# A float32 decoder trunk on one Trainium2 core: the MLP's up-projection by pairs of tiles, in seven block products in place of eight

## What is computed

```python
h = rmsnorm(x, mlp_norm[l])
u = jnp.square(jax.nn.relu(jnp.einsum('bsd,df->bsf', h, w_up[l])))    # 1024 -> 4096
x = x + jnp.einsum('bsf,fd->bsd', u, w_down[l]).astype(x.dtype)       # 4096 -> 1024
```

## Time and profile before

| | before |
|---|---|
| median of 3 runs (lowest, highest) | 1188.17 us (1187.81, 1190.7) |
| span of the profiled execution | 1186.0 us |
| busy PE / DVE / ACT / POOL | 1154.9 / 538.6 / 590.7 / 574.1 us |
| MLP of layer 0, of layer 1 (about) | 243 to 592 us, 824 to 1177 us |

### The profile page before, as it was taken

The page is one execution under the profiler, slowest core; times in us unless marked ns, Lnnn a source line. Parts: engine busy times, 40 slices in busy tenths (PEclk is TensorE's granted clock), DMA queues, the critical chain, the costliest instruction groups (busy, mean ns, idle before and its releaser), DMA issues.

```text
span 1186.0 us, 15497 instructions
## 1 busy us (share of the span) xinstructions
PE 1154.9 (97%) x5546; PEld 969.2 (82%) x5546; DVE 538.6 (45%) x783; ACT 590.7 (50%) x942; POOL 574.1 (48%) x310
## 2 busy tenths in 40 slices
PE   7999998999999999999999999899999999999996
PEld 5789887878888888888888889787888888888886
DVE  6766678654222222223355666758522222222224
ACT  5789898544133233134346888965422422322442
POOL 3454754664444444444744564456444444444452
PEclk9999999999999999999999999999999999999998
DMA  5220211223222323223222121012233232232222
GB/s 188 72 71 19 90 36 36 95 84 107 94 96 97 105 88 106 88 89 100 95 72 73 52 72 52 20 54 90 89 107 107 89 106 90 88 106 88 101 77 72
DMA packets 30027, 99.65 MB, mean 84 GB/s; under 512 B 3600, under 2 KB 5648, under 8 KB 29968
## 3 DMA queue, kind: packets, MB, share of 16 engines
q1 hardware_dynamic: 28992, 97.80, 24.6%
q10 hardware_dynamic: 976, 1.08, 0.3%
HBM read 96.77 MB, written 2.10 MB: 83 GB/s over the span
## 4 chain that ended last, share of the span: by engine, by line
PE 86%; ACT 7%; DVE 3%; issue 2%; ACTq 1%; DVEq 1%; DMA 0%
PE DW L441 24%; PE DW L443 23%; PE DW L442 23%; PE Z L441 2%; PE Z L443 2%; PE Z L442 2%; PE DW L528 2%; PE Z L594 1%; PE O L607 1%; PE Z L577 1%; ACTq L813 1%; ACT xm L786 1%; ACT work L814 1%; PE O L552 1%; ACT probs L853 1%
## 5 line engine op out<-in xcount | busy, mean ns | idle before, releaser
L955 POOL TENSOR_TENSOR w<-raw,w 128x1024 fp32r<-128x1024 f32 x178 | 429.1, 2413 | 410.4 <-ACT w L701 405.0
L701 ACT ACTIVATE w<-raw 128x1024 fp32r<-128x1024 f32 x177 | 185.7, 1051 | 226.8 <-PE DW L443 213.1
L441 PE MATMUL DW<-xm,w 128*128 128x512 f32 x512 | 200.2, 391 | 1.5 <-issue 1.5
L441 PE MATMUL DW<-stage,w 128*128 128x512 f32 x512 | 199.4, 389 | 0.6 <-DVE stage L1271 0.6
L443 PE MATMUL DW<-xm,w 128*128 128x512 f32 x512 | 199.2, 389 | 0.0
L442 PE MATMUL DW<-xm,w 128*128 128x512 f32 x512 | 199.2, 389 | 0.0
L443 PE MATMUL DW<-stage,w 128*128 128x512 f32 x512 | 199.2, 389 | 0.0
L442 PE MATMUL DW<-stage,w 128*128 128x512 f32 x512 | 199.2, 389 | 0.0
L1312 DVE TENSOR_TENSOR DW<-DW,probs 128x512 f32<-128x512 f32 x62 | 43.4, 700 | 224.5 <-PE DW L443 224.5
L1296 DVE TENSOR_TENSOR kf<-o 128x512 f32<-128x512 f32 x64 | 52.1, 814 | 204.0 <-ACT o L890 203.9
L441 PE MATMUL DW<-xa,w 128*128 128x512 f32 x296 | 119.1, 403 | 9.7 <-DVE xa L1073 7.6
(11 more groups left out here) (226 smaller groups left out, 1666.2 us busy)
## 6 DMA issues: line engine op xcount, KB each, us to landing
raw<-in_weights SPq DMA_DIRECT2D x179, 512.0 KB, 3.3
x<-in_x SPq DMA_DIRECT2D x6, 256.0 KB, 5.7
out_x<-x SPq DMA_DIRECT2D x6, 256.0 KB, 2.5
raw<-in_weights SPq DMA_DIRECT2D x2, 256.0 KB, 4.4
x<-in_x ACTq DMA_DIRECT2D x2, 256.0 KB, 5.0
out_x<-x ACTq DMA_DIRECT2D x2, 256.0 KB, 2.5
work<-in_positions SPq DMA_DIRECT2D x1, 256.0 KB, 6.7
gains<-in_gains ACTq DMA_DIRECT2D x1, 28.0 KB, 3.8
```

The lines of the kernel that those rows point to most:

```text
L441: pe.matmul(bank, w[:, slot, 0, k], rhs[:, 0, c], start=start, stop=False)
L701: act.activation(w[:, slot_of(l * PACKS + p), 0], raw[:, p % 2], ACT.Identity).then_inc(w_hi, 1)
L955: pool.tensor_tensor(w[:, slot, 1], raw[:, p % 2], w[:, slot, 0].bitcast(F32), ALU.subtract).then_inc(w_ready, 1)
```

## The change

The up tiles are taken in pairs. With the input features in two halves (top, bottom), the two output tiles of a pair and the 512 tokens in two halves of 256, a pair is a product of 2x2 blocks, and it is computed by Winograd's form of Strassen's scheme. Of a pair's weights DVE makes four sums in float32 (`weight_sum`, into `wsum`, 128x512 each, both inputs in SBUF); ACT and GpSimd then split seven granules of 128x512 (`split_up`; A and B are halves of the first tile, D a half of the second, S, T, U, V the sums). Of the input, four mixed blocks for each of the four chunks are made once for a layer (`gx`, `tf`, into `xa`). Each of the seven products is 4 chunks x 3 = 12 matmuls on 256 columns (`up_product`). They add up in three PSUM areas: A, T, S and V one after another in `acc_a`, with ACT copying a snapshot after A, T and S (steps VA, VB, VC), B in `acc_b`, U and D in `acc_d`; DVE joins area and snapshot (CA, CB, CD), ACT moves the fourth quarter with ReLU (VD), and DVE squares with ReLU in one instruction (CC, CD). UH and UL are the splits of u, as before. The first two tiles of each layer stay plain (PL), so a layer has 2 plain tiles and 15 pairs; the down tiles stay as they are, but use three banks. Steps are written out in strings, which each engine walks through, taking its own letters: P and D are PE's, K and J are splits of weights (J: for the next quarter), S and R the sums.

```diff
+OTHER_UP = '''
+PA0 SA1 SB1 PB0 VA0 KA1 SC1 PT0 KB1 CA0 SD1 PU0 VB0 KT1 PS0 KU1 PA1 VC0 KS1 CB0 PV0 VA1 KA2 PD0 VD0 KV1 CC0 SA2 SB2 SC2
+PT1 KD2 CD0 UH0 UL0 PU1 VB1 KT2 UH1 UL1 SD2 PB1 KU2 PS1 KB2 CA1 PA2 VC1 KS2 CB1 PV1 VA2 KA3 PD1 VD1 KV2 CC1 SA3 SB3 SC3
+'''
+UP_END = '''
+PT2 KD3 CD1 UH2 UL2 PU2 VB2 KT3 UH3 UL3 SD3 PB2 KU3 PS2 KB3 CA2 PA3 VC2 KS3 CB2 PV2 VA3 PD2 VD2 KV3 KP0 CC2
+PT3 CD2 UH4 UL4 PU3 VB3 KP1 UH5 UL5 PB3 KP2 PS3 CA3 DA0 VC3 CB3 PV3 VD3 CC3 PD3 DB0 UH6 CD3 DA1 DB1 UH7 UL6 UL7 DC0 DC1
...
+            def up_product(bank, weights_, part, start, ready=None):
+
+                for c in range(HC):
+                    if ready is not None:
+                        ready(c)
+                    pe.matmul(bank, weights_[:, c], part(0, c), start=start and c == 0, stop=False, skip_group_check=not start)
+                    pe.matmul(bank, weights_[:, c], part(1, c), start=False, stop=False, skip_group_check=not start)
+                    mm = pe.matmul(bank, weights_[:, HC + c], part(0, c), start=False, stop=c == HC - 1,
+                                   skip_group_check=not start)
+                mm.then_inc(p_done, 1)
...
-                    for c in range(KC):
-                        def ready(i):
-                            pe.wait_ge(xm_ready, l * KC + i + 1)
-                        p, tile = MLP_AT + c, MLP_TILE + c
-                        take(l, p, tile, q)
-                        products(slot_of(l * PACKS + p), D[:, (tile + 1) % 2], xm, range(KC), 0, True, True, ready if first and c == 0 else None
-                                 ).then_inc(tile_done, 1)
...
+                            elif kind == "S":
+                                pe.wait_ge(snapped, 3 * pair + 2)
+                                up_product(acc_a[n % 2], granule("S", n), lambda h, c: mixed(0, h, c), False)
+                            elif kind == "V":
+                                pe.wait_ge(snapped, 3 * pair + 3)
+                                up_product(acc_a[n % 2], granule("V", n), lambda h, c: xm[:, h, HC + c, HALF:], False)
...
+            def split_up(l, q, steps, step, m):
+
+                to, kind = granule(step[1], m), step[1]
+                pool.wait_ge(w_hi, split_count(l, q, steps, step, m))
+                pool.tensor_tensor(to[:, HC:], granule_from(kind, m), to[:, 0:HC].bitcast(F32), ALU.subtract).then_inc(w_ready, 1)
...
+            def weight_sum(l, q, steps, which, m):
+
+                top, low, pair = raws[2 * m % 4], raws[(2 * m + 1) % 4], pairs_before(l, q, m)
+                dst, a, b, op = {"A": (0, low[:, 0:HC], low[:, HC:], ALU.add),
+                                 "B": (1, wsum[:, 0], top[:, 0:HC], ALU.subtract),
+                                 "C": (2, top[:, 0:HC], low[:, 0:HC], ALU.subtract),
+                                 "D": (3, top[:, HC:], wsum[:, 1], ALU.subtract)}[which]
...
+                dve.tensor_tensor(wsum[:, dst], a, b, op).then_inc(wsum_ready, 1)
+                dve.drain()
...
+                    if 0 < d < 5:
+                        weight_sum(l, None, None, "ABCD"[d - 1], 1)
...
+                            dve.scalar_tensor_tensor(dst[:, 2], x[:, HC + n, HALF:], g, second, ALU.mult, ALU.subtract)
+                            dve.drain()
+                            dve.scalar_tensor_tensor(dst[:, 1], x[:, HC + n, HALF:], g, dst[:, 0], ALU.mult, ALU.subtract)
+                            dve.drain()
+                            dve.scalar_tensor_tensor(dst[:, 3], x[:, HC + n, 0:HALF], g, dst[:, 1], ALU.mult, ALU.subtract
+                                                     ).then_inc(t_sum, 1)
...
+                        elif step == "CD":
+                            dve.wait_ge(p_done, product_count(l, q, steps, "PD", n))
+                            dve.tensor_tensor(kf[:, 1, 0:HALF], acc_d[n % 2], saved_f[n % 2], ALU.add).then_inc(joined, 1)
+                            dve.drain()
+                            dve.scalar_tensor_tensor(kf[:, 1], kf[:, 1], 0.0, kf[:, 1], ALU.max, ALU.mult).then_inc(mlp_sq, 1)
```

More of the change, by code:

```diff
@@ L644, in quarter @@
                             add_norm(acc[:, 0, :], True, True).then_inc(w_full, 1)
-                    for d in range(down):
-                        def ready(i):
-                            pe.wait_ge(u_ready, l * QUARTERS * KC + q * KC + i + 1)
-                        p, tile = MLP_AT + KC + d, MLP_TILE + KC + d
-                        take(l, p, tile, q)
-                        products(slot_of(l * PACKS + p), D[:, (tile + 1) % 2], u, range(KC), 0, True, True, ready if d == 0 else None
-                                 ).then_inc(tile_done, 1)
@@ L662, in closing_products @@
+                quarter(None, FIRST)
+                with pe.Fori(1, QUARTERS - 1) as q:
+                    quarter(q, STEADY)
+                quarter(QUARTERS - 1, LAST[l])
             def closing_products(h, i):
[L664 to L665 removed]
+                d, l = CLOSING[i], DEPTH - 1
+                slot = slots[down_slot[d]]
                 if h == 0:
[L667 removed]
+                    pe.wait_ge(w_ready, split_count(l, QUARTERS - 1, LAST[l], "KP", d))
+                    pe.wait_ge(d_drained, l * DENSE + DOWN_TILE + (QUARTERS - 1) * KC + d)
@@ new lines, in split_up @@
+            def split_up(l, q, steps, kind, m, following):
+                at = q
+                if following:
+                    at = 1 if q is None else q + 1
+                if kind in "AB":
+                    act.wait_ge(raw_in[2 * m % 4], raw_count(l, at, 2 * m))
+                elif kind == "D":
+                    act.wait_ge(raw_in[(2 * m + 1) % 4], raw_count(l, at, 2 * m + 1))
+                else:
+                    act.wait_ge(wsum_ready, 4 * pairs_before(l, at, m) + 1 + "STUV".index(kind))
+                back = 2 if kind == "D" else 1
+                if following:
+                    act.wait_ge(p_done, product_count(l, q, steps, "P" + kind, m + UP_PAIRS - back))
+                    if kind in "AB":
+                        act.wait_ge(tile_done, l * DENSE + (0 if q is None else q * KC) + DOWN_TILE + 2 + 1 + CREDIT)
+                elif q is None and m - back < 1:
+                    tile = {"A": 1, "B": 1, "U": 5, "S": 5, "V": KC - 1}.get(kind, KC - 1 if kind == "D" and m == 2 else None)
+                    if tile is not None:
+                        act.wait_ge(tile_done, l * DENSE + SB_TILE + tile + 1 + CREDIT)
+                else:
+                    act.wait_ge(p_done, product_count(l, q, steps, "P" + kind, m - back))
+                act.activation(granule(kind, m)[:, 0:HC], granule_from(kind, m), ACT.Identity).then_inc(w_hi, 1)
@@ new lines, in snapshot @@
+            def snapshot(l, q, steps, step, m):
+                product, dst, src = {"VA": ("PA", saved_a, acc_a), "VB": ("PT", saved_f, acc_a), "VC": ("PS", saved_s, acc_a)}[step]
+                pair = pairs_before(l, q, m)
+                act.wait_ge(p_done, product_count(l, q, steps, product, m))
+                if not (q is None and m < 3):
+                    act.wait_ge(joined, 3 * (pair - 2) + {"VA": 1, "VB": 3, "VC": 2}[step])
+                act.activation(dst[m % 2], src[m % 2], ACT.Identity).then_inc(snapped, 1)
```

484 lines of the change are left out of this document (354 added, 130 removed).

## The result

The changed kernel takes **1257.11 us** (median of four runs, 1248.7 to 1258.12), the kernel before 1188.08 beside it: a ratio of **1.0558** (95% interval 1.0535 to 1.0581), so 69 us slower. The forecast was 1214.6 us in a range of 1170 to 1230: the side was right, the size was not, by 42 us. The profiled execution took 1256.14 us, its span is 1254.4.

The account below looks back on a forecast made before the run. The prediction took PE's matmul rate to bound the MLP. Matmuls -24.6, looped quarters +21 and MLP starts +30 summed to +26.4 us on 1188.2, giving 1214.6 us in a range of 1170 to 1230.

Parts of the forecast that it names:

- What bounds the kernel, and the exclusion: MLP runs at PE's matmul rate; two-SBUF-input DVE and GpSimd instructions do not run together, a pair costing the sum.
- The signs named beforehand: Sums and squares of 1.2 to 2 us; PE idle before V, before each layer's PT1, and in first plain tile.
- the sign of the sum: In the up stretches, busy GpSimd plus two-input DVE instructions come near 100% of the time.
- The matmuls: Up-tile pairs: 84 narrow matmuls replace 48 wide, 10.06 for 10.88 us; 0.82 saved a pair, 30 pairs, -24.6 us.
- Looped quarters: Three quarters in each layer: PE waits on GpSimd and DVE, 3.5 us a quarter, +21 us (4 to 27).
- The walk through a quarter: Row-by-row count of a looped quarter: V to V of 11.6 and 13.1 us, PE 4.5 late.
- the sum of the shared access: Up to a looped quarter's first down piece: GpSimd and DVE need 40.5 us against PE's 37.4, 3.1 late.
- The start of each MLP: Early sums +4, mixed blocks +6, rest of first quarter +5: +15 us a layer, +30 in all (14 to 42).
- The cover: Rival: DVE and GpSimd fall into step, looped quarters lose next to nothing; 1168 to 1184 us, chance 0.24.
- even: Rival: losses near the low bounds with one term at its middle; 1184.6 to 1191.8 us, chance 0.09.
- The narrow matmuls: Rival: each product's first matmul costs 0.1 us more, 21 us over 210 products; 1185 to 1195 us, chance 0.05.
- the last rival: Worse than forecast: cycle repeats in all pairs at 14 us, PE idles, its clock falls; 1230 to 1245 us, chance 0.09.

Follow-up runs that it names:

- no_port: Changed kernel with the quarters' sums, the squares of pairs 0 to 2 and low parts of u reading one input from PSUM: 1194.06 us.
- b_noport: Kernel before plus, per up tile outside first quarters, one GpSimd subtraction and four DVE instructions with one input in PSUM: 1197.58 us.
- sums_psum: Changed kernel with the sums of weights in the quarters reading one input from PSUM in place of SBUF: 1218.55 us.
- mix_psum: Changed kernel with the twelve 256-column instructions per layer for the mixed blocks reading one input from PSUM: 1245.31 us.
- early_psum: Changed kernel with the four early sums of weights ahead of each MLP reading one input from PSUM: 1251.36 us.
- b_half: Kernel before plus, per up tile outside first quarters, one GpSimd subtraction and one DVE instruction with two SBUF inputs: 1190.55 us.
- all_psum: Changed kernel with quarter sums, squares of pairs 0 to 2, low parts of u, 256-column mixed-block instructions and early sums reading one PSUM input: 1182.58 us.

## Why the prediction was wrong

**What bounds the kernel, and the exclusion: right.** That a two-input DVE instruction and one of GpSimd take turns was read from two places in the trace of before, and every run bears it out. The signs named beforehand are there: sums and squares of 1.2 to 2 us, PE idle before V (ACT's copy of S) and before T. So is the sign of the sum: GpSimd alone was busy 11.4 of the 13.2 us from V to V, but GpSimd or a two-input DVE instruction was running in 12.8 of them. One was named amiss: the first plain tile waits for a PSUM bank that DVE frees late, not for `xm`; it comes 2.3 and 2.9 us later for the 4 of the forecast. And the waits at D were not named.

**The matmuls: 24.6 forecast, 22 measured.** The looped quarters of no_port are 17.4 us shorter than before's, for 24 pairs: 0.73 a pair for 0.82. The rate is as read; 0.3 us a quarter goes at borders and where wide matmuls follow narrow ones.

**Looped quarters: the step that failed most, 3.5 us forecast, 7.6 measured.** All six lose 45.7 us (554.5 us, against 508.8 in no_port), not 21. The walk through a quarter was good: it had V to V at 13.1 us and PE 4.5 late, and the trace has 13.2, and 4.4 us lost up to the second V. The error was in what was made of it. The 4.5 was taken for the upper end, and a middle was taken because the sum of the shared access gave only 3.1. The sum itself came out: its work ends 41.2 us into the quarter (392.85) for 40.5, though with other terms (1.25 for a granule in place of 1.20, 0.45 for a DVE instruction between granules in place of 0.57, and GpSimd idle for 4.9 of the 28.0 us from 357 to 385, waiting for high parts). But it was set against PE's time at the end of the stretch, and PE waits in the middle, at V and D, for a chain over DVE. And the walk stopped at V: the D behind it waits 1.1 us for DVE's join, behind the fourth sum of the same chain, and the matmuls after the gaps lose 0.6. That makes 6.1, the figure of layer 1's first looped quarter (90.2 against 84.1; the second has 6.4). In layer 0's three the clock adds 2.3 each. The last quarter of layer 1 loses 8.2, with 7.9 of it in gaps; why its gaps are longer was not looked into.

**The start of each MLP: 15 forecast, about 21 measured** (15.9 and 16.5 in the first quarter, 2.3 and 2.9 for the late start, 2.2 for the three pairs' gain). The first plain tile 2.6 for 4. From the first plain tile to the first T it is 23.7 us in both layers where PE needs 14.2, so 9.5 are the mixed blocks', for 6: they were costed at 0.51 each, with 6 us of waiting in all. In layer 0's trace six of the twelve run one by one against granules and last 0.9 longer than alone, one lasts 1.9 longer, a low part of 1024 columns 0.9, and DVE waits 1.1 for ACT: 9.3. A short instruction waits as long as a long one when it waits for a whole granule. Behind the first T it is another 9 for 5, of which 3.3 lie before the first D (284.59), which waits for DVE's join; the rest was not taken apart.

**The clock: left out of the sum.** It stood only in the rival that was worse than forecast, with 0.09. It is worth 7 us of 42 in the profiled execution, all of it in layer 0's looped quarters.

**The rivals.** The cover does not hold: DVE and GpSimd do fall into step, 1.70 us a turn, and the quarters lose 7.6. Nothing came out even. The narrow matmuls keep their rate. What came was beyond the last rival, 1230 to 1245, which had the right elements (the cycle, idle pieces, the clock) and too low a price.

## What to carry to other kernels

When work moves from a full engine to idle ones, add up what the idle ones share: here seven granules on GpSimd and eight two-input DVE instructions a pair, each engine at two thirds of the span or less, and the mixed blocks cost some 74 us where 22 were to be gained. If a hand walk through the dependencies and a sum of loads give different lateness, the larger is the forecast and not the upper end (here 4.5 and 3.1, and 6.1 came), and the walk has to go on past the first wait. Where a wait hangs on two semaphores, check the profile's releaser against the program: the one that it names may have been there long before. A DVE operand in PSUM takes an instruction out of the exclusion: try it as an experiment first, to see what the exclusion is worth.

## What the runs showed of the hardware

- DVE and GpSimd exclude each other, but a turn does not cost the full sum: granules alternating with one DVE instruction of 0.69 us start 1.70 us apart (375.60, 377.31, 379.01 above), and in no_port 1.25 apart (360.78, 362.04, 363.29), so the DVE instruction adds 0.45. Its own record is 1.5 to 1.8 us.
- With one input in PSUM, a DVE instruction of 512 columns keeps 0.69 us beside a busy GpSimd (192 of them in b_noport with a mean of 692 ns, 42 in sums_psum with 689).
- The same pattern of waits of 0.9 to 1.7 us let TensorE's clock fall in one place and not in another. Two stretches of the changed kernel, layer 0 and layer 1, from the same V on:

```profile
385.00:402.00 17.00, 16.06 (x104) 15.59 (x105) 11.37 (x12) 7.32 (x13) 12.74 (x7) 0.80 0.43 134
1001.50:1018.50 17.00, 16.01 (x114) 14.95 (x115) 14.21 (x15) 8.22 (x15) 14.02 (x7) 1.00 0.46 154
```

It is not the layer: in mix_psum and early_psum the same quarter of layer 0, with the same waits, takes 90.2 us as in layer 1, not 92.5. What decides stays open; no run here was made for it. Nor was a mixture of pairs and plain tiles tried. By b_half, a load just under PE's time costs 2.7 us in all; but such a mixture would gain half of 22, and all_psum says that the start costs some 16 us even with most of its instructions off the shared access (22 gained, 5.5 left).
